# Streaming encoder step: keys of the running streams reordered, causal mask filled by VectorE in place of a product

## The reference

```python
def mla_attend(q, k, v, q_offset):
    ...
    s = jnp.einsum('bqhd,bshd->bhqs', qi, k).astype(jnp.float32) * scale
    s = jnp.where(k_chunk[None, :] <= q_chunk[:, None], s, -jnp.inf)   # CHUNK = 64 frames
    p = jax.nn.softmax(s, axis=-1).astype(v.dtype)
    return jnp.einsum('bhqs,bshd->bqhd', p, v)
```

## Time and profile before

| | |
|---|---|
| median of 3 runs | 620.95 us (620.64 to 622.15) |
| profiled execution, its own time | 620.64 us |
| span from first to last instruction | 618.9 us |
| TensorE busy | 599.2 us, 97% |
| VectorE busy | 369.4 us, 60% |
| ScalarE busy | 308.1 us, 50% |
| GpSimd busy | 109.8 us, 18% |
| granted TensorE clock, mean | 0.999 |
| chain that ended last | PE 70%, DVE 12%, ACT 10%, issue 3%, DMA 3%, POOL 2% |

### The profile page before, as it was taken

How to read it: one execution, slowest core, us unless ns; L and a number is a source line. 1 busy time by engine, 2 the same in 40 slices (tenths; PEclk the granted TensorE clock), 3 DMA queues, 4 the chain that set the end, 5 groups by cost and what they waited for, 6 DMA issues and landing times.

```text
span 618.9 us, 11804 instructions
## 1 busy us (share of the span) xinstructions
PE 599.2 (97%) x4546; PEld 576.6 (93%) x4546; DVE 369.4 (60%) x574; ACT 308.1 (50%) x616; POOL 109.8 (18%) x173
## 2 busy tenths in 40 slices
PE   8999999999999999999999999999999988799996
PEld 7999999999999999999999999989998977699996
DVE  5485667464554872277536478467788875663415
ACT  6796463442362562267326324345656567662311
POOL 0100010010030143156407200110000033400002
PEclk9999999999999999999999999999999999999999
DMA  8932362271262273242425222231110155856004
GB/s 299 348 97 87 101 204 78 73 216 54 78 203 70 79 271 104 61 147 87 135 51 156 69 69 61 60 90 31 35 53 18 51 172 203 252 176 238 1 2 170
DMA packets 65431, 73.46 MB, mean 119 GB/s; under 512 B 8160, under 2 KB 57568, under 8 KB 65248
## 3 DMA queue, kind: packets, MB, share of 16 engines
q1 hardware_dynamic: 65376, 72.71, 36.8%
HBM read 61.92 MB, written 10.78 MB: 117 GB/s over the span
## 4 chain that ended last, share of the span: by engine, by line
PE 70%; DVE 12%; ACT 10%; issue 3%; DMA 3%; POOL 2%; SPq 1%; DVEq 0%; ACTq 0%; POOLq 0%
PE bank L1598 22%; PE bank L1600 21%; PE bank L1599 21%; DVE pT_lo L1297 2%; DMA x_nat<-in_x_sample_dram 2%; ACT prob L1239 2%; DVE sT_lo L1297 1%; ACT slab_hi L1033 1%; DVE slab_lo L1297 1%; PE bank L1874 1%; ACT sT_hi L1033 1%; PE bank L1645 1%; DVE rows L1293 1%; DMA x_raw<-in_xT_dram 1%; ACT qS L1033 1%
## 5 line engine op out<-in xcount | busy, mean ns | idle before, releaser
L1598 PE MATMUL bank<-slab_hi,hat_hi 128*128 128x256 f32 (+2 forms) x560 | 160.4, 286 | 1.8 <-DVE hat_lo L1297 1.0
L1600 PE MATMUL bank<-slab_hi,hat_lo 128*128 128x256 f32 (+2 forms) x560 | 159.3, 285 | 0.0
L1599 PE MATMUL bank<-slab_lo,hat_hi 128*128 128x256 f32 (+2 forms) x560 | 159.3, 285 | 0.0
L1598 PEld LDWEIGHTS bank<-slab_hi,hat_hi 128*128 128x128 f32 x560 | 105.3, 188 | 3.3 <-DVE slab_lo L1297 1.4
L1600 PEld LDWEIGHTS bank<-slab_hi,hat_lo 128*128 128x128 f32 x560 | 105.6, 189 | 0.6
L1599 PEld LDWEIGHTS bank<-slab_lo,hat_hi 128*128 128x128 f32 x560 | 105.2, 188 | 0.6
L1297 DVE TENSOR_TENSOR slab_lo<-stage,slab_hi 128x1024 fp32r<-128x1024 f32 (+3 forms) x70 | 83.7, 1196 | 26.7 <-ACT slab_hi L1033 25.5
L1598 PE MATMUL bank<-hat_hi,slab_hi 128*128 128x320 f32 x256 | 79.4, 310 | 0.7 <-DVE krL L1297 0.4
L1599 PE MATMUL bank<-hat_lo,slab_hi 128*128 128x320 f32 x256 | 78.7, 308 | 0.0
L1600 PE MATMUL bank<-hat_hi,slab_lo 128*128 128x320 f32 x256 | 78.7, 308 | 0.0
L1033 ACT ACTIVATE slab_hi<-stage 128x1024 fp32r<-128x1024 f32 (+3 forms) x70 | 71.0, 1014 | 6.1 <-DMA stage<-in_a_w_in_dram 1.5
(11 more groups left out here) (324 smaller groups left out, 1369.7 us busy)
## 6 DMA issues: line engine op xcount, KB each, us to landing
stage<-in_a_w_in_dram SPq DMA_DIRECT2D x22, 512.0 KB, 4.6
st_s<-in_state_gla_dram SPq DMA_DIRECT2D x4, 1024.0 KB, 6.7
out_dram<-st_s SPq DMA_DIRECT2D x4, 1024.0 KB, 5.1
stage<-in_a_w_out_dram SPq DMA_DIRECT2D x8, 512.0 KB, 4.3
stage<-in_b_w_in_dram SPq DMA_DIRECT2D x8, 512.0 KB, 4.5
stage<-in_ckvT_dram SPq DMA_DIRECT2D x8, 512.0 KB, 4.0
stage<-in_cache_ckv_dram SPq DMA_DIRECT2D x8, 512.0 KB, 6.5
stage<-in_b_w_out_dram SPq DMA_DIRECT2D x8, 512.0 KB, 4.2
```

The source lines that it names most:

```text
L1598: pe.matmul(out, a[0], b[0], start=first, stop=False)
L1599: pe.matmul(out, a[0], b[1], start=False, stop=False)
L1600: return pe.matmul(out, a[1], b[0], start=False, stop=last)
```

## The change

Four things. The mask product leaves `S`; VectorE fills the masked corners of a unit's two tiles with the large negative value before it takes the maxima, and the two constants go (SBUF keeps their place as a pad). At the end of layer A, `xT` of tile 2 comes in front of `rs` of tile 4. In the heads, `ct` of streams 0 and 1 comes one head later, and `zr`, `cr` and `ot` of streams 0 and 1 come in front of `O` of head 5. In the turns of the streams `cr` and `ot` come in front of `ct`, weight pieces come at the end of a turn, and the halves of head 7's output (`Oh`) come in the first turn, behind the keys.

```diff
-CONST_R, NCONST_R = columns((("cum_p", P + 2), ("cum_s", P + 2), ("early", P), ("late", P)))
+CONST_R, NCONST_R = columns((("cum_p", P + 2), ("cum_s", P + 2)))
...
+        if NT <= t < NT + 3:
+            out += [("xT", "B", t - 3)]
         if t == NT:
             out += [("rs", NT - 1)]
-        if NT <= t < NT + 3:
-            out += [("xT", "B", t - 3)]
...
+        if h == 5:
+            out += [("zr", 0), ("cr", 0), ("ot", 0), ("cr", 1), ("ot", 1)]
         if h == 6:
             out += [("cr", 2), ("ot", 2), ("ss", 0)]
         if h >= 0:
-            out += [("O", h)] + [("Oh", h)] * (h != 6)
+            out += [("O", h)] + [("Oh", h)] * (h < 6)
...
-        if h in (3, 4):
-            out += [("ct", h - 3)]
-        elif h == 5:
-            out += [("zr", 0), ("cr", 0), ("ot", 0), ("cr", 1), ("ot", 1)]
+        if h in (4, 5):
+            out += [("ct", h - 4)]
...
     for b in range(SB):
         out += [("st", b)] + [("zr", b + 2)] * (b + 2 < SB)
-        if b in (2, 4):
-            out += [("piece", ("wo", "B", 0), b // 2 - 1)]
-        elif b in (5, 6):
-            out += [("piece", "uv", b - 5)]
-        elif b == 7:
-            load(("wo", "B", 1))
         if b + 3 < SB:
-            out += [("ct", b + 3), ("cr", b + 3), ("ot", b + 3)]
+            out += [("cr", b + 3), ("ot", b + 3), ("ct", b + 3)]
+        if b == 0:
+            out += [("Oh", HB - 1)]
...
         out += [("sv", b), ("cs", b)]
+        if b in (2, 4):
+            out += [("piece", ("wo", "B", 0), b // 2 - 1)]
+        elif b in (5, 6):
+            out += [("piece", "uv", b - 5)]
+        elif b == 7:
+            load(("wo", "B", 1))
...
         const_r = sb("const_r", [P, NCONST_R], fp32r)
+        place[0] += 8 * P
...
                 elif kind == "S":
                     _, h, u = step
+
+                    i0, i1 = UNITS[u]
+                    apart = 512 + (i1 - i0) * P
+                    link(dve.memset(row[0:P // 2, i0 * P:i0 * P + 2 * apart].rearrange("p (j n) -> p j n", n=apart)[:, :, P // 2:P], NEG))
                     for j, i in enumerate(UNITS[u]):
...
                         pe.matmul(o, qS[:, h, q], krS[:, keys], start=False, stop=False)
-                        pe.matmul(o, qS[:, h, q], krL[:, keys], start=False, stop=False)
-
-                        last = pe.matmul(bank[:, j, q], cst_r("early"), cst_r("late"), start=False, stop=True)
+                        last = pe.matmul(o, qS[:, h, q], krL[:, keys], start=False, stop=True)
```

More of the change, by code:

```diff
@@ L1912, in constants @@
     ang = (pos[:, None] * inv[None, :]).reshape(NT, P, RH).transpose(1, 0, 2).reshape(P, NT * RH)
-    row = (i == 0).astype(np.float32)[:, None]
     const = [np.eye(P), before, before * same, (i[:, None] // SL % 2 == np.arange(2)[None, :]), np.cos(ang), np.sin(ang)]
-    const_r = [cum_p, cum_s, row * (1 - half.T * 0 - (i >= P // 2)[None, :]), row * np.where(i >= P // 2, NEG, 0.0)[None, :]]
+    const_r = [cum_p, cum_s]
     return [np.ascontiguousarray(np.concatenate(x, axis=1).astype(np.float32)) for x in (const, const_r)]
```

## The result

The changed kernel takes 625.12 us (median of 16 runs, 622.56 to 626.89); the kernel before, run beside it on the same chips, 622.17 us (16 runs, 620.44 to 625.85). The ratio of the two, taken over the runs, is 1.0042, 95% interval 1.0028 to 1.0056: slower by 2.6 us (1.7 to 3.5), where the forecast had +2.5. The two medians alone are 2.95 apart, which lies in that interval. The profiled execution has a span of 621.4 us and a time of 623.22.

The account below looks back on a forecast made before the run. From head 2's scores on, the loop between VectorE and ScalarE was taken as the bound, also in the streams' turns. Terms -0.6 + 2.0 - 1.25 + 0.3 + 1.65 + 0.75 + 0.35 - 0.7 gave +2.5: 623.4 us, range 621.5 to 625.5.

Parts of the forecast that it names:

- Mask product, heads 0 and 1: Scores of heads 0 and 1, where TensorE leads: removing the mask products saves time, -0.6 us.
- Fills: Heads 2 to 7: each head's first VectorE mask fill lies on the path at 0.33 us, +2.0 (ends +1.0 and +3.3).
- the second is hidden up to 0.40: Each head's second fill only delays VectorE's 0.40 us idle time, so costs nothing if a fill takes less than 0.40.
- Head 3's keys: Stretch from 470.08: without latent keys it shrinks from 12.92 to a plain 11.67 us, -1.25.
- Head 5: Rotary copies move into ScalarE's idle time, latent keys replace them, +0.3; two low halves share with GpSimd, +0.35 (0 to 0.9).
- Turns of the streams: Rotary copy delays five turns 0.65 each, head 7's output +0.05, weight pieces -0.4, less 1.25 slack: +1.65 us.
- Sharing with GpSimd: Streams' turns: VectorE's latent low half is held by GpSimd's product, 0.15 us a turn (0.07 to 0.22), +0.75 over five.
- Layer A: Layer A's end: transposed tile 2 split earlier removes waits, part given back by later squares, -0.7 us (0 to -1.0).
- Loads and constants: Staged loads reordered, landing before use; smaller constant copy on GpSimd and SBUF pad: 0 us.
- copies at no cost: Streams' turns: rival that the copies in front cost nothing since supposed path is idle; 621.0 us, chance 0.12.
- GpSimd as the bound: Streams' turns: rival that GpSimd sets the pace, so TensorE's 5.0 us of waits go; 616.0 us, chance 0.08.
- TensorE as the leader of later heads: Later heads: rival that TensorE leads, fills hidden and 6 x 0.29 us saved; 619.7 us, chance 0.08.

Follow-up runs that it names:

- piece_behind: The changed kernel, but GpSimd's product on head 4's weight piece waits for VectorE's divisions of head 0; 622.70 us, 1.0028 against the kernel before.
- mask_only: The kernel before with only the mask part changed: mask products out, VectorE's fills in; 621.99 us, ratio 1.0015.
- rotary_first: The kernel before with only rotary keys and the streams' own keys put before the latent keys in the five turns having them; 624.85 us, 1.0060.
- gpsimd_behind: The changed kernel, but in the streams' turns GpSimd's rotary low half waits for VectorE's latent low half; 624.15 us, 1.0047 against the kernel before.

## Why the prediction was right, by its own steps

The time, 623.4 against a median of 620.95, was +2.5; the measured ratio makes 2.6 of that median. The terms are less good than the sum: two of them were 0.4 too low and one 0.5 too high, and that they cancel is luck.

- **Mask product, heads 0 and 1: -0.6.** Mis-sized twice. Without the collision it is -0.9 (piece_behind, mask_only); in the change 0.7 of it is lost to GpSimd's piece, so -0.2. The forecast looked for GpSimd and VectorE side by side only where a step had been moved.
- **Fills: +2.0.** +1.5, between the forecast's ends. One is 0.28 in five of the heads and 0.10 in one (446 to 457), where VectorE had idled 0.22 us between a reciprocal and its division and no longer did. The statement that the second is hidden up to 0.40 fell: its cover stands in front of the second unit's exponentials, and one fill fills it. It cost next to nothing here because it just fits.
- **Head 3's keys: -1.25.** -1.25. **Head 5: +0.3 and +0.35 of sharing.** +0.49 together. `skS` stands in idle time as said; of two low halves beside GpSimd one took 1.44.
- **Turns of the streams: 0.65 each, +0.05, -0.4, less 1.25 of slack.** From the end of the exponentials ahead of the first to the copy ahead of the full stretch it was 29.99 us and is 33.44: +3.45, where 2.9 + 0.75 = 3.65 was forecast; less slack +2.3 at 544, forecast +2.4. The mechanism was right. Two sizes were off and cancel: the copies with their sharing cost 4.2 (rotary_first, five turns) where 0.65 and 0.15 a turn make 4.0, and the pieces at the turn's end give 0.8 (7.67 and 7.70 became 7.26 and 7.29) where 0.4 was forecast. Whose the slack is was not known: it belongs to the pieces, and with the order of keys as before they give -1.5 with it.
- **Sharing with GpSimd: 0.15 a turn.** 0.10 (gpsimd_behind).
- **Layer A: -0.7.** -0.3. The step "TensorE is led by nothing else until the heads" held, and the 0.7 was there at 300 us. It was then eaten by TensorE itself, whose tiles took 4.96 instead of 4.87; gpsimd_behind, without that, has the -0.7.
- **Loads and constants: 0.** No turn shows a late load. But only a late load was thought of: one that landed a microsecond sooner put GpSimd's piece beside the division, and that is the 0.7 of the first item.

Sum of the measured: -0.3 - 0.2 + 1.5 - 1.25 + 0.5 + 2.3, and 0.15 inside the full stretch, is +2.7. The rivals: copies at no cost and GpSimd as the bound fall with rotary_first. TensorE as the leader of later heads falls with mask_only, whose heads grew by 0.28 where it would have made them shorter. But GpSimd was not without say: it led TensorE's last scores in the kernel before.

## What to carry to other kernels

A step moved in front of another on the same engine costs its full length if the only gap of the loop lies behind it; order matters by where the gap is, and not by which data are wanted first. Idle time in front of one instruction is not the cover for an addition upstream: follow each reader of what is delayed, and take the smallest slack. A change whose halves don't add up has a collision in it: the table of the same product's starts in each half and in the whole finds the stretch, the rows of that stretch the place, and one added wait tests it.

## What the runs showed of the hardware

- A VectorE fill of 64 partitions by 128 elements in PSUM, each waited for, has a row of 0.17 us, but one more makes a head 0.25 longer, and two in a row have 0.42.
- A GpSimd cast of 32 elements on each partition takes 0.21 us alone and 1.08 when VectorE's low half with both inputs in SBUF is running. Two divisions of VectorE with up to 384 columns went from 0.68 together to 1.25 beside a GpSimd product of 0.88 us. Both sides can be held.
- In the changed kernel TensorE's granted clock was 0.50 of full speed from 506 to 509 us, that is the lower of its two levels, after 3 us in which TensorE had been busy 1.50; in the kernel before and in piece_behind it stayed at 1.00 there. The products around 508 came 1 us late by it, and nothing at 544 did: piece_behind is ahead of the changed kernel by the same 0.7 us at 504 and at 544.
- TensorE's pace is not always the same at granted clock 1.00 and without a wait. One full stretch (224 to 276 us) was 2.0 us longer in two of the fourteen profiled executions: 87 products in 10 us instead of 90 or 91. And the four tiles after 303 us took 4.96 us each instead of 4.87 in eight. What held it is open.
